# Dense up-projection with gathered dot products in place of seven-product blocks, in a one-core PEER trunk

## What is computed

```
q = (h @ w_q)                      # 8 heads, product keys, top 16 of 128 x 128 experts
u = u_table[experts]               # 16384 rows of 2048
act = gelu(einsum('btd,btrkd->btrk', h, u))
y = einsum('btrk,btrkd->btd', gates * act, v_table[experts])
h = layer_norm(alpha * h + y + ple)
```

## Time and profile before

| what | value |
|---|---|
| median of 3 runs | 3961.21 us |
| span of the profiled execution (no other time was taken of that execution) | 3962.2 us |
| PE busy | 3896.8 us (98%) |
| DVE busy | 2842.4 us (72%) |
| POOL busy | 2273.4 us (57%) |
| ACT busy | 1330.7 us (34%) |
| moved by DMA | 943.27 MB, mean 238 GB/s |

### The profile page before, as it was taken

One profiled execution on the slowest core, in us unless ns is written; L12 is line 12 of the kernel. 1 busy time (PEld: TensorE's weight loads), 2 busy tenths in 40 slices (PEclk: granted clock), 3 DMA queues, 4 the chain that ended last, 5 costly groups with the idle time before them and its releaser, 6 DMA issues.

```text
span 3962.2 us, 59722 instructions
## 1 busy us (share of the span) xinstructions
PE 3896.8 (98%) x21569; PEld 3382.9 (85%) x21569; DVE 2842.4 (72%) x3796; ACT 1330.7 (34%) x1577; POOL 2273.4 (57%) x1162
## 2 busy tenths in 40 slices
PE   6999999999999999999999999999999999999998
PEld 5788888888887888888999999999987888888886
DVE  7555555566623459997777777777537999999998
ACT  3233233342213322234444444444323333333332
POOL 6343344434442345446877777788107788787771
PEclk9999999999999999999999999999999999999999
DMA  6555555543442326687888888875549999999994
GB/s 239 189 198 198 198 192 187 194 160 138 159 167 72 117 85 244 234 279 230 243 240 239 239 239 244 245 224 139 192 178 355 375 387 390 383 391 374 391 383 190
DMA packets 385875, 943.27 MB, mean 238 GB/s; under 512 B 104136, under 2 KB 186072, under 8 KB 319736
## 3 DMA queue, kind: packets, MB, share of 16 engines
q1 hardware_dynamic: 177624, 593.08, 41.3%
q0 software_dynamic: 88064, 176.47, 14.2%
q10 hardware_dynamic: 120096, 172.59, 12.6%
HBM read 846.85 MB, written 263.97 MB: 280 GB/s over the span
## 4 chain that ended last, share of the span: by engine, by line
PE 45%; issue 31%; POOL 14%; DVE 7%; DVEq 1%; ACT 1%; DMA 1%; POOLq 1%; SPq 0%; ACTq 0%
POOL wlo L772 13%; PE bank L1670 8%; PE bank L1672 8%; PE bank L1671 8%; PE bank L1728 5%; PE bank L1730 5%; PE bank L1729 5%; DVE wlo L1757 2%; DVE res L2395 2%; PE bank L1389 1%; PE bank L1391 1%; PE bank L1390 1%; ACT whi L1358 1%; DVE res L2414 1%; DVEq L2412 1%
## 5 line engine op out<-in xcount | busy, mean ns | idle before, releaser
L772 POOL TENSOR_TENSOR wlo<-raw,whi 128x1024 fp32r<-128x1024 f32 x296 | 768.7, 2617 | 995.1 <-ACT whi L954 463.6
L834 POOL DMA_INDIRECT gates_d<-sel_g,place_u x384 | 754.9, 1966 | 209.9 <-DMA gates_d<-sel_g,place_u 120.0
L1389 PE MATMUL bank<-h_hi,whi 128*128 128x512 f32 x1712 | 674.4, 394 | 1.9 <-POOL wlo L772 1.3
L1391 PE MATMUL bank<-h_hi,wlo 128*128 128x512 f32 x1712 | 666.9, 390 | 0.0
L1390 PE MATMUL bank<-h_lo,whi 128*128 128x512 f32 x1712 | 666.3, 389 | 0.0
L1728 PE MATMUL bank<-whi,ew_hi 128*128 128x512 f32 x1408 | 550.1, 391 | 14.6 <-DVE wlo L1757 14.6
L1730 PE MATMUL bank<-whi,ew_lo 128*128 128x512 f32 x1408 | 548.5, 390 | 0.0
L1729 PE MATMUL bank<-wlo,ew_hi 128*128 128x512 f32 x1408 | 548.5, 390 | 0.0
L1670 PE MATMUL bank<-h_hi,p_hi 128*128 128x256 f32 x1600 | 452.9, 283 | 0.4 <-DVE p_lo L1757 0.4
L1671 PE MATMUL bank<-h_lo,p_hi 128*128 128x256 f32 x1600 | 452.8, 283 | 0.0
L1672 PE MATMUL bank<-h_hi,p_lo 128*128 128x256 f32 x1600 | 452.8, 283 | 0.0
(11 more groups left out here) (336 smaller groups left out, 7991.9 us busy)
## 6 DMA issues: line engine op xcount, KB each, us to landing
raw<-in_weights SPq DMA_DIRECT2D x338, 1024.0 KB
v_rows_d<-in_weights ACTq DMA_DIRECT2D x96, 1024.0 KB
x_raw<-in_weights SPq DMA_DIRECT2D x50, 1024.0 KB
parts_d<-in_weights SPq DMA_DIRECT2D x32, 1024.0 KB
v_rows_d<-in_weights SPq DMA_DIRECT2D x32, 1024.0 KB
gates_d<-zeros SPq DMA_DIRECT2D x32, 768.0 KB, 10.4
act_d<-mt ACTq DMA_DIRECT2D x128, 192.0 KB
act_in<-act_d SPq DMA_DIRECT2D x64, 384.0 KB
```

Source lines behind the costliest of these rows:

```text
L772: pool.tensor_tensor(wlo[slot][:, part], raw[slot][:, part], whi[slot][:, part].bitcast(F32), ALU.subtract).then_inc(lo_made, 1)
L834: pool.indirect_dma_start(out=places_d, out_offset=bass.IndirectOffsetOnAxis(ap=place_u[:, t, k:k + 1], axis=0), in_=sel_g[:, t, k:k + 1], ...
L1389: pe.matmul(bank[:, :], whi[slot][:, cols], rhs_hi[:, c, :], start=c == 0, stop=False)
L1391: last = pe.matmul(bank[:, :], wlo[slot][:, cols], rhs_hi[:, c, :], start=False, stop=c == DC - 1)
```

## The change

**U stage.** The seven-product blocks are gone. All 128 slabs are plain blocks over tokens 0 to 383 only (384 columns). POOL makes `wlo` of slabs 0 to 15, DVE of the other 112. For the last 128 tokens, whose 128 picks each are known by then, POOL gathers the picked rows of U (`gather_u`, 128 x 8 KB each) and DVE takes the dot product with the token's own row (`dot`).

**Row table of U.** The slabs hold U with the width on the partitions, so rows are made on the chip: DVE turns a slab in 32 x 32 blocks (`turn_slab` or `turn_unit`, 128 x 2048 elements a slab) and SP stores it to `u_rows_d` in four DMAs (`store_rows`). 81 slabs are turned before the U stage: 53 in the heads, 16 in Up, 12 in Out, each with 1 MB more loaded by SP (`table_step`). The other 47 (slabs 16 to 62) are turned in the U stage from the slab that is there anyway.

**POOL.** 200 scatters, then 128 gathers with the other 184 scatters between them, 3 to every 2 gathers. A scatter waits only once in 16. The gathers wait for the whole table.

**Moved and removed.** `lay_parts` and `parts_d` are gone; a part row is taken from the weights and its activation from `act_d`, so `pick_part` goes. `lay_rows`: 32 issues in the heads as before, then 8 in GLU, 28 in the query stage, 32 in Gate and 28 in the U stage (before: 96 in the U stage). The attention output goes by DRAM. `h1_hi`, `h1_lo` are laid out by token tile. The saves and loads of `res` and of `h1` around the U stage are gone.

```diff
-U_PLAIN, U_LATE = 16, 12
+U_POOL = 16
+FIRST_SCATTERS = 200
+def scatters_before(k):
+    return min(TD * PICKS, FIRST_SCATTERS + (3 * k + 1) // 2)
+def dot_slab(k):
+    return 67 + 4 * k // 7
...
+            def table_step(x):
+                if x > 0:
+                    sp.wait_ge(tr_made, 2 * x)
+                if x < STEPS:
+                    for h in range(2):
+                        sp.dma_start(tin[h][:, :], weights[AT_U + step_slab(x), :, HALF * h:HALF * (h + 1)]
+                                     ).then_inc(tin_landed[h], 16)
+                if x > 0:
+                    store_rows(tout, step_slab(x - 1), tout_stored)
...
+            for n in range(FIRST_SCATTERS):
+                scatter(n)
+            pool.wait_ge(tables_made, 1)
+            pool.wait_ge(tout_stored, 64 * (STEPS + 1))
+            for k in range(2):
+                pool.wait_ge(tab_stored[k], 64 * TURNED[k])
             for k in range(PICKS):
...
+                gather_u(k)
+                for n in range(scatters_before(k), scatters_before(k + 1) if k + 1 < PICKS else TD * PICKS):
+                    scatter(n)
...
+            pool.wait_ge(u_used, PICKS)
+            pool.wait_ge(blk_done, BLK_V)
             gather_row(0)
...
             for o in range(N_GATE):
                 next_hi(AT_GATE, o // 2, o % 2, blk_done, BLK_GATE + o)
+                for c in range(2):
+                    lay_rows(act, HEADS + N_GLU // 2 + N_Q // 2 - 1 + o // 2, 2 * (o % 2) + c)
...
+            def turn_slab(x):
+                dve.wait_ge(tout_stored, 64 * x + 64)
+                for h in range(2):
+                    dve.wait_ge(tin_landed[h], 16 * x + 16)
+                    dve.transpose(out=tout[:, :, 8 * h:8 * h + 8, :].rearrange("p e c i -> p c e i"),
+                                  in_=tin[h][:, :].rearrange("p (c e j) -> p c e j", c=8, e=4)).then_inc(tr_made, 1)
...
+            def dot(k):
+                dve.wait_ge(u_row_landed[k % U_ROWS], 16 * (k // U_ROWS + 1))
+                dve.scalar_tensor_tensor(u_row[k % U_ROWS][:, :], u_row[k % U_ROWS][:, :], 1.0, h_tok[:, :], ALU.mult,
+                                         ALU.mult, accum_out=act_p[:, k:k + 1]).then_inc(u_used, 1)
+            for e in range(U_POOL, N_U):
+                if e in TURN_U:
+                    turn_unit(e)
+                low_part_of(e - U_POOL, e % 2, raw[e % 2])
+                while dots < PICKS and dot_slab(dots) <= e:
+                    dot(dots)
+                    dots += 1
+            for k in range(dots, PICKS):
+                dot(k)
```

More of the change, by code:

```diff
@@ L316, in build_trunk @@
+    gate_p, gate_c = sel_g[:, TD, :], sel_g[:, T_PART, :]
+    w_c = w("w_c", [P, PICKS], 38)
+    part_row = [w(f"part{i}", [P, 512], 30 + 2 * i) for i in range(ROWS)]
     end_hi = whi + [sb("whi2", [P, SL], a_at + 32 * kb, F32R)]
@@ L492, in _ @@
             sp.wait_ge(band_laid, 16)
-            with sp.Fori(0, HEADS) as i:
+            for i in range(HEADS):
                 sp.wait_ge(ef_made, i + 1)
@@ L630, in load_aux, with load_unit @@
+            def load_unit(e, landed):
+                sp.wait_ge(dve_lo_made, e - 2 - U_POOL + 1)
+                sp.dma_start(raw[e % 2][:, :], weights[bass.ds(AT_U + e, 1), :, :].rearrange("a p n -> (a p) n")
+                             ).then_inc(landed, 16)
+            for e in range(U_POOL + 2, N_U + 1):
+                load_unit(e, raw_landed[e % 2])
+                if e - 2 in TURN_U:
+                    store_rows(u_tout[e % 2], e - 2, tab_stored[e % 2])
             def load_aux(J, q):
@@ L996, in head @@
                 step(1)
+                if not begins:
+                    act.wait_ge(ya_stored, 16 * i)
                 act.activation(q_h[:, :], ps_p[1][:, :], copy).then_inc(qkv_made, 1)
@@ L1093, in next_hi @@
                     act.activation(whi[slot][:, part], raw[slot][:, part], copy).then_inc(hi_made, 1)
-            with act.Fori(0, N_GLU // 2) as j:
+            for j in range(N_GLU // 2):
                 for s in range(2):
@@ L1128, in _, with queries @@
             up_pair(DC // 2 - 1, True)
-            def queries(start, end, more=None):
+            def queries(start, end, more=None, lays=True):
                 with act.Fori(start, end) as j:
@@ L1346, in expert_pair @@
+            with act.Fori(U_LAYS, SB) as j:
+                experts(j, False)
+            act.wait_ge(u_used, PICKS)
+            act.activation(act_p[:, :], act_p[:, :], ACT.Gelu_apprx_tanh).then_inc(acts_made, 1)
             def expert_pair(J, nxt, last):
@@ L1662, in _ @@
-            with pe.Fori(0, U_PLAIN // 4) as j:
+                    pe.wait_ge(evac, EV_U + e + 1)
+                    block_of(beside(ps_u[s % 2], TD), s % 2, AT_U + e, lambda c: tokens(h1_hi, c, TD),
+                             lambda c: tokens(h1_lo, c, TD), None, e - U_POOL if by_dve else None)
+            with pe.Fori(0, U_POOL // 4) as j:
                 experts(j, False)
-            def product(region, k, right):
-                hi, lo = right
-                for c in range(WC):
-                    cols = slice(c * P, (c + 1) * P)
-                    pe.matmul(region, p_hi[k][:, cols], hi[:, c, :], start=c == 0, stop=False)
-                    pe.matmul(region, p_hi[k][:, cols], lo[:, c, :], start=False, stop=False)
-                    last = pe.matmul(region, p_lo[k][:, cols], hi[:, c, :], start=False, stop=c == WC - 1)
-                last.then_inc(prod_done, 1)
@@ L1881, in _, with mixer_head, slot @@
             dve.wait_ge(bb_made, 1)
[L1883 removed]
+            def turn_slab(x):
+                dve.wait_ge(tout_stored, 64 * x + 64)
+                for h in range(2):
+                    dve.wait_ge(tin_landed[h], 16 * x + 16)
+                    dve.transpose(out=tout[:, :, 8 * h:8 * h + 8, :].rearrange("p e c i -> p c e i"),
+                                  in_=tin[h][:, :].rearrange("p (c e j) -> p c e j", c=8, e=4)).then_inc(tr_made, 1)
+            def mixer_head(i, begins):
+                def slot(r):
+                    if not begins or r >= 3:
+                        turn_slab(7 * i + r - 3)
                 dve.wait_ge(pv_done, i + 1)
@@ L2003, in split @@
                 return tt(lo, src, hi.bitcast(F32), ALU.subtract)
-            with dve.Fori(0, WC // 2) as j:
+            for j in range(WC // 2):
+                if j == 2:
+                    attention_lo()
                 for s in range(2):
@@ L2045, in _ @@
             for g in range(3):
+                for n in range(4):
+                    turn_slab(HEAD_STEPS + UP_STEPS + 4 * g + n)
                 dve.wait_ge(blk_done, BLK_OUT + 4 * g + 4)
```

694 lines of the change are left out of this document (222 added, 472 removed).

## The result

The kernel after took 4161.24 us (median of 4 runs, 4158.28 to 4168.57), the kernel before 3962.45 (3960.39 to 3964.01) beside it: 1.0504 times as long, 95% interval 1.0491 to 1.0517. Forecast were 3933 and at most 4035, so the change is 199 us slower where it was expected to be 28 faster. The profiled execution spans 4161.5 us against 3962.2.

A forecast was written before the change was run, and what follows sets the result against it. PE was taken to bound every stage before, POOL's chain to set U's end after. 3961 - 45 (U) - 10 (V) + 27 (before U) = 3933 us; own range 3895 to 3985, with rivals 3820 to 4035.

The forecast's parts named there:

- Step 1, PE's own work: U stage: 6144 matmuls of 384 columns at 0.172 us, 1058 us; with PE the bound, 258 us less.
- rival D: U stage: fewer columns don't shorten a matmul, 0.225 us each, +78 us, 4056 in all; chance 0.02.
- Step 2, start and end of POOL's chain: U stage: POOL's chain sets the end; it starts 124 us in, and 12 us follow the last gather.
- rival A: U stage: the port shared with DVE costs POOL little; 164 us less, 3814 in all; chance 0.20.
- Step 2, first 200 scatters: U stage, scatters ahead of the gathers: 2.15 us each, together 430 us, ends 368 to 500.
- Step 2, gathers with scatters: U stage: 128 gathers with 184 scatters; 107 at 5.60 us, the last 21 at 5.07; 705 us.
- Step 3, V: V stage: `pick_part` goes, 10 of PE's 14.6 us lost to late low parts come back; ends 0 and 20.
- Step 4, transposes and traffic: Stages before U: turns of 2.4 us a slab and the table's DMA traffic cost +27 us, ends 0 and 121.
- Out: DVE is idle for whole blocks; 0: Out stage: the turns cost 0 us, since DVE has idle blocks there.
- Hidden, with little to spare: Heads: turns in the scan and softmax fit the time before PE asks; +3 us in all, ends 0 and 40.
- a sign of being wrong: Start of the U stage: beginning 60 us or more later than 1654 would show full DMA queues before it.
- Rival B: Stages before U: full DMA queues bring slabs late and DVE stands at turns; +121 us, 4027 in all; chance 0.20.

The follow-up runs named there:

- the kernel that had them at 1.00: Kernel after with every load and store of the early table steps kept, but only the first slab turned and no wait for later turns; 4063.9 us.
- the kernel with later dots: Kernel after with a second turn buffer, two turns moved ahead of the bias adds, dots and low parts in halves, first dot at slab 78 (before 67); 4030.4 us.

## Why the prediction was wrong, step by step

- **Step 1, PE's own work:** right, 0.173 us against 0.172, so rival D falls.
- **Step 2, start and end of POOL's chain:** right. The first scatter came at U + 130 (forecast 124), and V's first weights 10.9 us after the last gather (12). That this chain sets U's end was right too, with a hole in PE of 105 us before V (3068.9 to 3173.9; forecast 90 to 110); rival A falls.
- **Step 2, first 200 scatters:** "Each is 1.54 + 0.31 + 0.30 = 2.15, together 430" was mis-sized by 89 us. Without the stores it is 2.15 to 2.18, so the sum was right for a kernel that doesn't store. Missing was a term for the 47 MB of stores in the same stretch, worth 83 us. I had the price of a slab's store (3.0 us of all engines) from the heads and used it only ahead of U.
- **Step 2, gathers with scatters:** "5.60 together" measured 6.08. The lock was sized well in sum, 1.60 us a gather where 0.70 x 2.44 = 1.71 were charged. What the sum lacked is again the gaps, 0.46, and it averaged the scatters over all gathers (1.44) where 1.50 stand behind each of the first 107, another 0.11. The last 20 came at 5.06 against 5.07, which is luck: 1.15 scatters each in place of 1.44 made up for 0.50 us of gaps, nearly all waits for row buffers. Over all 128, 705 became 752. With 130 and 10.9 for the ends: 1271 + 6 + 89 + 47 - 1 = 1412.
- **Step 3, V:** -2 in place of -10. PE's late low parts did go from 14.6 to 2.4 us. The first weight load of V (8.5 us on the chain) and the clock regained only after the hole are seen at its start; what they cost wasn't tried.
- **Step 4, transposes and traffic:** the turn cost 2.37 us (2.4 forecast) and the bytes were sized well enough: Gate ran at 1.05 of the engines and 399 GB/s and lost 6 us of the 15 allowed. The failing sentence is "Out: DVE is idle for whole blocks; 0", with "Hidden, with little to spare" for the heads. Both priced the turn's own time. The diff had the wait on `tout_stored` ahead of each turn and SP's on `tr_made` ahead of each load, and I never walked round that ring: 9.5 + 2.4 us. Heads, GLU, Up and Out came to 101 us and not 12. U began 108 us later than 1654, which the prediction had named as a sign of being wrong.
- **Rival B** had its direction but not its cause. It had DVE stand at a turn, but for a slab that full queues bring late, and put +121 on that; DVE stood for the landing of the stores. The loss came with the engines' share at 0.85 in Up (947 to 1121) and 0.66 in Out (1121 to 1400), and it was gone in the kernel that had them at 1.00.

As a sum: 3933 + 141 in U + 81 ahead of it + 8 in V = 4163, against 4161.5.

## What to carry to other kernels

A single buffer that is filled, stored and waited for has a period, the fill plus the landing of its stores; compare that period with the block it is meant to hide under before comparing the fill alone, and see what stands in order behind the wait. The same holds for the buffers of gathered rows. Indirect DMAs want quiet on the DMA queues as well as on DVE: add up the transfers of every stretch in which they are issued, including stores that nobody waits for. Where an engine has to wait for another's chain in any case, let it do its own part and its bulk traffic first, and wait at the end.

## What the runs showed of the hardware

- **Not every DVE instruction holds up POOL.** Turns of 128 x 2048 float32 (2.3 us each) cost the scatters beside them nothing: 121 in 250 us with DVE busy 129 us or 69. Low parts and dots, which read two inputs, do: a scatter beside a dot took 3.28 us where 1.54 is its least. The Trainium skill, "SBUF — State Buffer", section "SBUF: two separate sides", takes only two-port modes and operations with two SBUF inputs as lock holders, the latter against a GpSimd operation that reads SBUF. These rows agree, if an indirect DMA, which reads its indices there, counts as one; so rival A's reading of the page was the wrong one.
- **Bulk traffic stops POOL between instructions, not within them, and the DMA share alone doesn't say how much.** With the row table's stores most scatters beside them kept 1.54 us, and gaps of 2.6 to 3.6 us stood between them, at a share of 0.97; without them, at 0.58, the scatters' mean gap was 0.33. But at 0.90, with the stores in larger pieces, it was 1.16, and at 0.98 with no such stores (2400 to 2700 of the kernel with later dots) 0.53. What POOL stands for in the gap no row names.
- **Full DMA engines did not slow PE.** A stretch at share 1.00 and 359 GB/s kept 442 matmuls in 100 us.
- **The size of the pieces mattered little.** Stores in pieces of 8 KB in place of 2 KB took the share in U from 0.97 to 0.90 and left the scatters no faster (2.67 us against 2.60).
- **One core alone moved 399 GB/s** in late Gate. "DMA: Bandwidth & Descriptors" of the Trainium skill, section Specifications, gives 358 GB/s as the HBM limit per core, as half of what two cores share; the measurement is above it.
